# Two transformer blocks in one kernel: the weight ring's low part is written over its raw part, and loads wait for TensorE

## What is computed

```python
def first_block(x, meta_tokens, ...):            # 16 meta tokens in front: 528 positions
    h = concat([meta, x])
    h = h + 0.5 * rmsnorm(swiglu(rmsnorm(h, g1), w_gate, w_up, w_down), g2)      # width 2816
    m = hybrid_mixer(rmsnorm(h, g3), ...)        # stick-breaking + latent attention, two gates, w_out
    h = h + rmsnorm(m, g4)
    h = h + 0.5 * rmsnorm(swiglu(rmsnorm(h, g5), ...), g6)
    return h[:, 16:]

def second_block(x, p, positions, ...):
    for layer in range(2):
        h = rms_norm(x, norm_mix[layer])
        mix = rglru_mlstm_mixer(h, ...) if layer == 0 else swa_sink_mixer(h, positions, ...)
        x = x + mix
        x = x + conv_ffn(rms_norm(x, norm_ffn[layer]), w_up, conv_w, conv_b, w_down)   # width 3072
        gate = sigmoid(rms_norm(x, norm_ple[layer]) @ ple_w_gate[layer])
        x = x + gate * (p[layer] @ ple_w_proj[layer])
    return x
```

## Time and profile before

| | |
|---|---|
| median of three runs | 2628.61 us |
| profiled execution, its own span | 2629.4 us |
| TensorE busy | 2557.5 us, 97% |
| VectorE, ScalarE, GpSimd busy | 1287.1, 936.0, 1007.0 us |
| mean granted clock of TensorE | 0.988 of full |
| DMA, mean over the span | 84 GB/s, 25.3% of the 16 engines for the weights |
| GpSimd's low parts (L292) | 425 times, 2.356 us each |
| ScalarE's high parts (L285) | 425 times, 1.011 us each |

### The profile page before, as it was taken

One profiled execution on the slowest core, in us unless ns is written; L12 is line 12 of the kernel. 1 busy time (PEld: TensorE's weight loads), 2 busy tenths in 40 slices (PEclk: granted clock), 3 DMA queues, 4 the chain that ended last, 5 costly groups with the idle time before them and its releaser, 6 DMA issues.

```text
span 2629.4 us, 34816 instructions
## 1 busy us (share of the span) xinstructions
PE 2557.5 (97%) x13322; PEld 2116.4 (80%) x13322; DVE 1287.1 (49%) x1396; ACT 936.0 (36%) x1310; POOL 1007.0 (38%) x445
## 2 busy tenths in 40 slices
PE   7999998999999999999999999999999999999999
PEld 7999998955777788888677688888877678888887
DVE  4433104367446534420487866663175745666213
ACT  4222223176334342222465232222254543222223
POOL 4444443302223344444343444444443124444443
PEclk9999999989999999999999999999999999999999
DMA  4222232201112222223321132223222012222321
GB/s 169 91 88 78 84 97 86 81 11 51 55 57 72 81 96 96 96 83 93 98 81 57 64 104 96 96 96 105 99 85 84 29 41 97 98 98 98 105 97 64
DMA packets 66048, 220.54 MB, mean 84 GB/s; under 512 B 8289, under 2 KB 8545, under 8 KB 65826
## 3 DMA queue, kind: packets, MB, share of 16 engines
q1 hardware_dynamic: 63792, 216.99, 25.3%
q10 hardware_dynamic: 2162, 2.25, 0.3%
HBM read 216.58 MB, written 2.10 MB: 83 GB/s over the span
## 4 chain that ended last, share of the span: by engine, by line
PE 88%; DVE 7%; ACT 3%; issue 2%; DMA 0%; ACTq 0%; SPq 0%; DVEq 0%
PE PS L297 26%; PE PS L298 26%; PE PS L299 26%; DVE acc L496 1%; PE PS L2792 1%; ACT xh L470 1%; PE PS L1258 1%; DVE h L566 1%; PE PS L1610 1%; DVE xl L474 1%; PE PS L1243 1%; PE PS L2773 0%; DVE sq L488 0%; PE PS L2811 0%; DVE mt L1795 0%
## 5 line engine op out<-in xcount | busy, mean ns | idle before, releaser
L292 POOL TENSOR_TENSOR wlo<-wraw,whi 128x1024 fp32r<-128x1024 f32 (+2 forms) x425 | 1000.4, 2356 | 1560.5 <-ACT whi L285 1559.9
L297 PE MATMUL PS<-xh,whi 128*128 128x512 f32 (+2 forms) x2504 | 893.8, 357 | 37.8 <-DVE xl L474 19.7
L299 PE MATMUL PS<-xh,wlo 128*128 128x512 f32 (+2 forms) x2504 | 882.6, 352 | 0.0
L298 PE MATMUL PS<-xl,whi 128*128 128x512 f32 (+2 forms) x2504 | 882.3, 352 | 0.0
L285 ACT ACTIVATE whi<-wraw 128x1024 fp32r<-128x1024 f32 (+2 forms) x425 | 429.2, 1011 | 844.7 <-PE PS L299 833.7
L297 PEld LDWEIGHTS PS<-xh,whi 128*128 128x128 f32 (+1 forms) x2504 | 473.2, 189 | 110.3 <-DVE xl L474 23.5
L299 PEld LDWEIGHTS PS<-xh,wlo 128*128 128x128 f32 (+1 forms) x2504 | 473.6, 189 | 63.6 <-issue 0.5
L298 PEld LDWEIGHTS PS<-xl,whi 128*128 128x128 f32 (+1 forms) x2504 | 473.7, 189 | 60.5 <-issue 1.2
L297 PE MATMUL PS<-hid2h,whi 128*128 128x512 f32 x560 | 217.8, 389 | 0.0
L298 PE MATMUL PS<-hid2l,whi 128*128 128x512 f32 x560 | 217.8, 389 | 0.0
L299 PE MATMUL PS<-hid2h,wlo 128*128 128x512 f32 x560 | 217.8, 389 | 0.0
(11 more groups left out here) (415 smaller groups left out, 3255.0 us busy)
## 6 DMA issues: line engine op xcount, KB each, us to landing
wraw<-w_up_dram SPq DMA_DIRECT2D x96, 512.0 KB, 3.2
wraw<-w_dn_dram SPq DMA_DIRECT2D x48, 512.0 KB, 3.2
wraw<-w_f1gu_dram SPq DMA_DIRECT2D x44, 512.0 KB, 3.3
wraw<-w_f2gu_dram SPq DMA_DIRECT2D x44, 512.0 KB, 3.2
wraw<-w_hyin_dram SPq DMA_DIRECT2D x24, 512.0 KB, 3.3
wraw<-w_win_dram SPq DMA_DIRECT2D x18, 512.0 KB, 3.3
wraw<-w_gate_dram SPq DMA_DIRECT2D x16, 512.0 KB, 3.3
wraw<-w_pg_dram SPq DMA_DIRECT2D x16, 512.0 KB, 3.3
```

Source lines behind the costliest of these rows:

```text
L292: pool.tensor_tensor(wlo[:, s, 0:size], wraw[:, s, 0:size], whi[:, s, 0:size].bitcast(F32), ALU.subtract).then_inc(lo_done.s, 1)
L297: pe.matmul(out_, whi[:, s, a:b], xhi, start=start, stop=False, skip_group_check=True)
L298: pe.matmul(out_, whi[:, s, a:b], xlo, start=False, stop=False, skip_group_check=True)
L299: return pe.matmul(out_, wlo[:, s, a:b], xhi, start=False, stop=stop, skip_group_check=True)
```

## The change

`wlo` is placed at the address of `wraw`: the subtraction reads the raw chunk and writes the low part over it. The third ring is no longer there; 16 KB per partition stay unused. As TensorE now reads that slot too, SP waits for `chunk_used` of chunk g-4 before it loads chunk g, in both places where it issues weight loads. No instruction is added, removed or moved in any engine's order; only the address and the awaited semaphore are others.

```diff
--- before.py
+++ after.py
@@ -132,7 +132,7 @@
         assert o_end <= 56800 * 4, o_end
         wraw = at("wraw", o_raw, [P, RING, SLOT])
         whi = at("whi", o_hi, [P, RING, SLOT], F32R)
-        wlo = at("wlo", o_lo, [P, RING, SLOT], F32R)
+        wlo = at("wlo", o_raw, [P, RING, SLOT], F32R)
         h = at("h", o_h, [P, DT, TK])
         xh = at("xh", o_x, [P, DT, TK], F32R)
         xl = at("xl", o_x + 4 * DT * TK, [P, DT, TK], F32R)
@@ -270,7 +270,7 @@
             s, rnd, g = slot_of(base, k, per_body, j)
             size = CHUNK_SIZE[base + k]
             if base + k >= RING:
-                sp.wait_ge(*lo_done(g - (RING - 1)))
+                sp.wait_ge(*chunk_used(g - (RING - 1)))
             return s, size
 
         def split_hi(act, base, k, per_body=RING, j=0):
```

## The result

The changed kernel takes 2676.6 us in the median of four runs (2669.14 to 2686.06), the kernel before 2627.97 (2623.35 to 2628.64). The ratio is 1.0193, 95% interval 1.0179 to 1.0208 (the plain quotient of the two medians is 1.0185): slower by 48.6 us, where 42 were forecast. The profiled execution of the changed kernel spans 2673.9 us against 2629.4.

What follows compares the result with a forecast made beforehand. TensorE was taken as the bound (88% of the span). Boundary waits 37.2, gaps given back -3.1, norm interference +0.9, clock +6.8 make 41.8; 2628.6 + 41.8 = 2670 us, range 2656 to 2686 (8 in 10: 2649 to 2691).

Steps and rivals of the forecast that it cites:

- plain streaming stays covered: Gate/up, down, conv-up, output projections: 6.9 us from slot release to usable chunk fits in three chunks' 16.3 us; no loss.
- L547 later: Logarithm in the norm after f1dn, behind a split waiting for its load: +2.6 us; three such norms, 7.8 us.
- window: Handover from qkv to window attention: logarithm L2647, right behind a split, starts later, +3.37 us.
- mLSTM: Handover from hyin to mLSTM: same shift of ScalarE's work less some 1.1 us of slack, +2.3 us.
- embedding gate: First embedding stage: table loads, root and sine behind a split start later, and VectorE's chain with them, +3.0 us.
- Openings: Stage starts where slots come free nearly together: win +2.5, f2gu +3.0, hyin +3.7, qkv +2.4 us; sum 11.6.
- The term of -3.1: Three TensorE gaps behind VectorE operations stretched by GpSimd's low parts (1.56, 1.20, 0.35 us) close: -3.1 us.
- 6.8 were forecast for the clock: New or longer TensorE gaps lower its clock: four half-clock stretches at 1.7 us each, +6.8 us.
- its eight places: Gaps of 2.0 to 4.5 us that might lower the clock: four openings, mix, mLSTM, window, embedding gate; 0 to 27 us.
- The rival without clock loss: Whole kernel: the same waits but no half-clock stretches added, 2664 us; chance 0.24.
- win to stick: Handover from win to stick-breaking: four copies L1145 behind a split start later, TensorE waits, +3.05 us.
- latent: Handover from projections to latent attention +2.0 us; 15 splits before exponentials within latent attention +1.0 us.

Runs made afterwards that it cites:

- experiment 2: Kernel before (three rings), with loads waiting for TensorE's use only from chunk 8 on in the long stages: 2627.17 us, ratio 1.0004 to the kernel before.
- 3: Kernel before (three rings), with loads waiting for TensorE's use only in each stage's first eight chunks and in short stages: 2675.83 us, ratio 1.0196.
- experiments 1: Changed kernel with the low part given its own ring again, the late load waits kept: 2677.25 us, ratio 1.0205 to the kernel before.

## Why the prediction was right, and where it was not

**Bound and place.** The forecast that plain streaming stays covered (6.9 us against 16.3) is shown by experiment 2, and that the price lies at the boundaries by 3. The sizes of the single shifts (L547 later by 2.37 us of 2.6, window 3.3 of 3.37, mLSTM 2.3 of 2.3, TensorE's wait in f2gu 2.84 of 3.0, the whole step there 3.8) followed from one load time and one queue.

**A place that was missed.** The prediction says that it went through all stage boundaries, but the latent projections are not in its list, with no reason given. They hold a split too, behind the second head; it waited for its load and the head's copy behind it, which releases a bank, came late:

```profile
635.08 1.06 ACT L285 ACTIVATE whi<-wraw 128x1024 fp32r<-128x1024 f32 x1 [4.56 <-DMA wraw<-w_ukv_dram]
...
637.33 0.47 PE L297 MATMUL PS<-ch,whi 128*128 128x512 f32 x1 [2.75 <-ACT qm L1503]
```

Here the timeline's idle before L285 is 4.56 us, for this load landed 5.1 us after its issue at 629.97. No other weight load was under way (the next was issued at 634.66), but ScalarE's queue had issued a copy of 528 KB, km<-kro, at 627.85, which took until 632.94; the packets of the weight load start only at 632.0. In the kernel before, no weight load fell on that copy. At the embedding gate the load took 4.8 us (the split's idle there is 4.37 us), again with no other weight load under way; what held it is not shown. That made this place dearer than 3.0: its first scaling ran 4.5 us later, TensorE waited 3.73 us for x6l, and a stretch at lower clock followed, 5.7 in all.

**Openings.** They cost 15.0 instead of 11.6. The forecast priced the fifth chunk well in win and f2gu and the root too low: in win it stood behind four splits that each waited for a load, and TensorE lost another 1.9 us to it. It gave each of these loads 3.3 us, but they overlap: in win they landed 3.1, 4.4, 5.3 and 5.1 us after their issue. In hyin 2.2 us were lost at the fifth chunk and 2.95 behind it, of which 1.6 to a lower clock (below).

**What was to be given back.** The term of -3.1 failed in sign at one of its three gaps. Mix and conv-up 1 gained 2.3 and 0.6. The root before conv-up 0 did not. The last square (L488) is held by a low part in both kernels, and in the changed one a low part also holds a sum before it. The kernel before, VectorE and TensorE:

```profile
1520.59 2.88 DVE L488 TENSOR_TENSOR sq<-h 128x512 f32<-128x512 f32 x1
...
1524.25 0.70 PE L511 MATMUL PS<-acc,con 128*128 128x512 f32 x1 [1.20 <-DVE acc L496]
```

VectorE, GpSimd and TensorE of the changed kernel:

```profile
1548.90 2.89 DVE L474 SCALAR_TENSOR_TENSOR xl<-h,vec,xh 128x512 fp32r<-128x512 f32 x1
...
1554.28 2.85 DVE L488 TENSOR_TENSOR sq<-h 128x512 f32<-128x512 f32 x1
...
1554.18 2.40 POOL L292 TENSOR_TENSOR wlo<-wraw,whi 128x1024 fp32r<-128x1024 f32 x1 [2.94 <-ACT whi L285]
...
1557.91 0.70 PE L511 MATMUL PS<-acc,con 128*128 128x512 f32 x1 [2.53 <-DVE acc L496]
```

The gap of 1.20 us became 2.53. The sum at 1548.90 took 0.74 us in the kernel before.

**Clock.** The cores' rows give a mean granted clock of 0.988 before and 0.985 after, which is 80 us at half clock (2 x 0.015 x 2673.9) against 63 (2 x 0.012 x 2629.4), 17 more. TensorE works through part of that only, so it costs at most half, 8.5 us; the gaps over 0.9 us grew by 39.3 us in all (39.3 to 78.6), which leaves 5 of the 44.5 us for the clock and small waits, where 6.8 were forecast for the clock; with the small gaps counted, 3.4 are left. The windows of the changed kernel around the openings of f2gu and, at the embedding gate's end, of qkv (columns as in the earlier trace rows):

```profile
950.00:954.40 4.40, 1.62 (x8) 1.00 (x6) 0.00 (x0) 2.01 (x2) 2.34 (x1) 1.00 0.83 270
954.40:957.80 3.40, 3.34 (x15) 2.76 (x16) 0.00 (x0) 1.79 (x3) 3.14 (x3) 1.00 0.39 145
...
2007.80:2011.50 3.70, 0.01 (x1) 0.01 (x1) 3.48 (x5) 2.86 (x5) 2.87 (x2) 0.93 0.01 2
2011.50:2015.00 3.50, 3.50 (x9) 2.81 (x10) 3.47 (x3) 0.00 (x0) 2.77 (x1) 0.58 0.00 0
```

A gap of 2.84 us kept the clock at 1.00, one of 3.73 was followed by 0.58. But the length of the gap does not decide it. Behind the wait of 1.90 us in the opening of hyin the changed kernel has the first row, where the same products in the kernel before have the second:

```profile
1331.20:1335.00 3.80, 3.80 (x10) 3.04 (x11) 0.00 (x0) 2.40 (x3) 3.77 (x2) 0.57 0.28 113
...
1303.80:1308.00 4.20, 4.20 (x19) 3.29 (x18) 0.62 (x1) 3.48 (x4) 4.20 (x3) 1.00 0.66 211
```

The part of a step that is not idle time is 1.9 us in hyin, 1.9 at the embedding gate, 1.8 at the entry of mix and 1.7 in the latent projections, the forecast's price of 1.7 four times, though the projections were not among its eight places; against it stand -2.2 in stick-breaking and -2.4 after mLSTM, where single profiles differ as much. The rival without clock loss (2664) lies below the measured interval, but the waits were mis-sized by nearly as much, so it falls by these rows and not by the time. I ran nothing that holds the clock apart, so its share stays an estimate.

**The sum.** Projections, gate and openings were too small by 10 us and the root gap by 3; win to stick and latent were too large by 3, and the clock, whose 6.8 us already lie in the steps, takes up the rest: 44.7 against 41.8. So the nearness of the number is in part luck: the waits were put at 35.0 us (37.2 - 3.1 + 0.9) where TensorE's idle time grew by 40.9, and the clock at 6.8 where 3.4 are left for it.

The medians differ by 48.6 where the two profiles differ by 44.5. A run's time is 1.7 us above its span, so the profile of before belongs to a run of some 2631.1 us (an estimate), 3.1 above the median of 2627.97, and that of the changed kernel, 2675.6 us, lies 1.0 below its median. The four runs of the changed kernel lie between 2669 and 2686 us, a wider spread than before's, and the slowest has the lowest mean granted clock (0.981, against 0.983 and twice 0.985). The kernels of experiments 1 and 3 show the same: their runs above 2683 us have 0.982, the others 0.983 to 0.985.

## What to carry to other kernels

Before a buffer's release is moved later, do not ask whether the ring still covers the load on average; list what stands in the queue of the engine that waits for the load, at each change of stage, and price each place with one load time. Where several slots come free together, count more than one load, and look for other transfers that the later load will now meet. And look at the slack as well as at the loss: a stage that now loses 0.4 us may lose 60 with a load that lands 2.7 us later, up to 26 of them through the clock.

## What the runs showed of the hardware

Doubling the bytes on the 16 DMA engines (25.3% to 45.6% of their time in the kernel before) did not lengthen the kernel before: ratio 1.0004. A load of 512 KB landed in 3.2 us in the median, in 5.3 us when issued 0.6 us behind another of its size, and in 5.1 us when issued 2.1 us behind a copy of 528 KB. A GpSimd subtraction of 1024 columns in place took what it took out of place (2.328 and 2.356 us), and in two halves 1.27 and 1.32 us, so a second instruction costs 0.26 us, less than what it saves VectorE and TensorE here: 11 us over the kernel, in either form.
